# Sparse attention in ten units in place of fourteen: joined local branches, one compressed unit for all heads, values by blocks

## The chip, the cores and the metric

The kernel runs on one core of a Trainium2 chip. The metric is the device time of one execution in microseconds (us). Three runs of the kernel before gave 896.19 to 897.03, median 896.92.

## The reference

Two transformer layers run one after the other on 256 tokens with 1,024 features, in float32. The first (stick-breaking attention, gated linear attention, a feed-forward part) is not touched. In the second the mixing has three branches: sparse attention, a convolution of 31 taps over 512 channels, and attention over 256 memory tokens. Their outputs are gated and added, and a feed-forward part follows. The sparse attention has 8 query heads of 64 features in two groups that share keys and values, and three branches of its own:

```python
s_c = einsum(qq, kc); p_c = masked_softmax(s_c, cmp_end <= t)      # 15 compressed blocks
o_c = einsum(p_c, vc)
...
s_s = einsum(qq, k_g); p_s = masked_softmax(s_s, tok <= t)         # selected blocks
...
s_w = einsum(qq, kwb); p_w = masked_softmax(s_w, m_w)              # window of 512
return gg[..., 0:1] * o_c + gg[..., 1:2] * o_s + gg[..., 2:3] * o_w
```

With 256 tokens there are four blocks to select from and up to 16 may be selected, and the window of 512 covers all that is past. So the selected and the window branch each are causal attention over all tokens, with keys and values of their own; these two are the local branches. The compressed keys and values come from a two-layer network over blocks of 32 tokens.

## The kernel before

All weights pass through a ring of three chunks of 128x2048 elements. SP loads a chunk, ScalarE (ACT) casts it to its high part (`split_hi`, L1383), VectorE (DVE) subtracts to get the low part (`split_lo`, L1984), and TensorE (PE) multiplies high and low parts (three products for each tile; L648 to L650). The second layer's mixing is a loop over steps, one for each chunk, written out for each engine: step s handles chunk number s from `kcvc` on (0 kcvc, 1 ca0, 2 cg0, 3 kk, 4 wk0, 5 q0, 6 wk1, 7 q1, 8 wv0, 9 vv, 10 wv1, 11 ca1, 12 cg1, 13 qm0, 14 qm1, 15 to 24 halves of the gates, 25 to 28 output projections). The chunks `wk` and `wv` (L1109) belong to the compressing network and their products are short; those of the others take about three times as long. In step s an engine first does what the chunk needs and then, in fixed places, pieces of attention and of other small work. Every engine works its queue strictly in that order.

Attention is cut into units, listed in `ATT`; unit i begins in step `ATT_AT + i`, with `ATT_AT` 8. A unit is one branch of one group of four heads for one tile of 128 query tokens (s selected, w window, c compressed), or the memory attention of one tile (m): s, s, w, w, c, c for tile 0, the same for tile 1, then two m, 14 in all. Its pieces are:

- step of the unit: PE's scores (`att_scores`, L1175, m L1167; the mask is added by a product with the identity, L1182); VectorE's maximum over the keys (`att_max_`, L2437, and a small instruction L2438); ScalarE's exponentials with their sums (`att_exp`, L1787, one for each head);
- one step later: reciprocal, gate and scaling of the weights (`att_scale`; VectorE L2445 to L2460, or ScalarE L1796 for the units in `SCALED_BY_ACT`);
- two steps later: PE turns the weights, one block of 128x128 at a time (`att_turn`, L1197); ScalarE copies them out (`att_evac`, L1804);
- three steps later: PE multiplies with the values (`att_values`, L1233, for c L1228, for m L1216), for two units at a time; after the last branch of a tile ScalarE and VectorE write high and low parts of the output (`att_out`, L1815 and L2473).

Scores of all units use the same two PSUM banks, so scores i wait until the exponentials of unit i-1 are done; turns use two other banks and wait for the copy before. VectorE puts the convolution's 124 taps (`conv_taps`, L2494, one 128x256 instruction each) at the end of each step; `TAPS_AT` says how many in which step. On VectorE the order in a step is: scaling of unit i-1, maximum of unit i (in the first two steps of attention these two stand the other way round), normalizations, `split_lo` of the chunk three steps ahead, output, taps. In step 8, 12 it also finishes the hidden product of the compressing network (L2551 to L2553); step 13 on PE projects the compressed values (L1303), and ScalarE copies them out (L1891). In step 15 ScalarE loads another table of functions (L1365).

```python
ATT = [(k, a, g) for a in range(TT) for k in "swc" for g in range(2)] + [("m", a, 0) for a in range(TT)]
SCALED_BY_ACT = (6, 7, 8, 9, 12, 13)
ATT_AT = 8
TAPS_AT = [0, 0, 0, 0, 2, 2, 2, 0, 0, 0, 6, 5, 8, 6, 7, 8, 8, 9, 9, 14, 8, 9, 8, 13]
```

Of the kernel before, what the change touches and what calls it, by code (L numbers as in the profile page):

```python
# [7 lines left out]
F32 = mybir.dt.float32  # L8
# [23 lines left out]
def two_block_kernel(  # L32
# [98 lines left out]
    ATT = [(k, a, g) for a in range(TT) for k in "swc" for g in range(2)] + [("m", a, 0) for a in range(TT)]  # L131
    SCALED_BY_ACT = (6, 7, 8, 9, 12, 13)
    ATT_AT = 8

    with ExitStack() as ctx:
# [136 lines left out]
        vc = AR[0:15, 8854:8982].rearrange("p (g n) -> p g n", g=2)  # L272
# [19 lines left out]
        amax = TMP[:, 4382:4438].rearrange("p (u h) -> p u h", h=4)  # L292
        aden = TMP[:, 4438:4494].rearrange("p (u h) -> p u h", h=4)
        acoef = TMP[:, 4494:4550].rearrange("p (u h) -> p u h", h=4)
# [124 lines left out]
        def key_tiles(i):  # L419
            kind, a, g = ATT[i]  # L420
            return 2 if kind == "m" else 1 if kind == "c" else a + 1

        def group_of(i):

            kind, a, g = ATT[i]
            return 4 + a if kind == "m" else 2 * a + g

        def att_out_bank(i):
            kind, a, g = ATT[i]
            return PS[:, 6 + a, :] if kind == "m" else PS[64 * g:64 * g + 64, 6, :]  # L430
# [82 lines left out]
        def _(pool):  # L513
# [119 lines left out]
            for i in range(2):  # L633
# [8 lines left out]
                               pattern=[[P, TT], [-16, 15]], channel_multiplier=1).then_inc(mask2_made, 1)  # L642

        @block.tensor
        def _(pe):
# [502 lines left out]
            def att_scores(i):  # L1148
                kind, a, g = ATT[i]
                if i >= 1:  # L1150
                    pe.wait_ge(att_e, 4 * i)
# [6 lines left out]
                if i == 4:  # L1158
                    pe.wait_ge(fn_made, 4)
                if i == 12:  # L1160
# [4 lines left out]
                for h in range(4):  # L1165
                    if kind == "m":
                        mm = pe.matmul(PS[:, h // 2, (h % 2) * T:(h % 2) * T + T], qm[:, h, tok], kmT[:, h, :],  # L1167
                                       start=True, stop=True)
                        continue
                    r = slice(64 * (h % 2), 64 * (h % 2) + 64)  # L1170
                    q = qn[r, 2 * g + h // 2, tok]

                    L = 15 if kind == "c" else P * (a + 1)
                    k = kcT[r, 15 * g:15 * g + 15] if kind == "c" else kdup[kind][r, g, 0:L]
                    pe.matmul(PS[:, h % 2, h // 2 * L:(h // 2 + 1) * L], q, k, start=h < 2, stop=False, skip_group_check=True)  # L1175
                if kind != "m":
                    m = mask_r[:, P + 30 * a:P + 30 * a + 30] if kind == "c" else mask_r[:, 0:P].unsqueeze(1).to_broadcast([P, 2, P])
                    for e in range(2):
                        z = PS[:, e, 0:2 * L]
                        if kind != "c":  # L1180
                            z = z.rearrange("p (h n) -> p h n", h=2)[:, :, P * a:P * a + P]
                        mm = pe.matmul(z, ident_r[:, :], m, start=False, stop=True, skip_group_check=True)  # L1182
                mm.then_inc(att_s, 1)

            def att_turn(i):
# [8 lines left out]
                L = 15 if kind == "c" else P  # L1194
                for s in range(key_tiles(i)):
                    for h in range(4):
                        mm = pe.transpose(PS[0:L, 2 + s, h * P:(h + 1) * P],  # L1197
                                          pbuf[:, i % 2, (h * key_tiles(i) + s) * L:(h * key_tiles(i) + s + 1) * L],
                                          ident[:, :])
                mm.then_inc(att_t, 1)  # L1200

            def att_values(i):
# [3 lines left out]
                if kind == "m":  # L1206
                    if a == 0:
                        pe.wait_ge(att_lo, 4)
                    else:
                        pe.wait_ge(vc_made, 1)  # L1210
# [12 lines left out]
                if kind == "s" and a == 1:  # L1223
                    pe.wait_ge(att_lo, 2)
                if kind == "c":
                    pe.wait_ge(vc_made, 1)
                    for w in range(2):
                        pe.matmul(att_out_bank(i - 1 + w), vc[:, w, :], pT[0:15, w, 0:512], start=False, stop=True,  # L1228
                                  skip_group_check=True).then_inc(att_o, 1)
                    return  # L1230
                for s in range(key_tiles(i)):
                    for w in range(2):
                        mm = pe.matmul(att_out_bank(i - 1 + w), vn[kind][:, s, 64 * w:64 * w + 64],  # L1233
                                       pT[:, w, s * 512:(s + 1) * 512], start=kind == "s" and s == 0, stop=False,
                                       skip_group_check=True)
                        if s == key_tiles(i) - 1:
# [15 lines left out]
            for s in range(FFN2 - B2 - 4):  # L1252
# [5 lines left out]
                elif name.startswith("o"):  # L1258
                    br = "mcn".index(name[2])
                    if name[3] == "0":  # L1260
                        if br == 0:
                            pe.wait_ge(att_lo, 6)
                        elif br == 1:
                            pe.wait_ge(cv_lo, 1)
                        else:
                            pe.wait_ge(att_lo, 4)
# [32 lines left out]
                if s == 13:  # L1299
                    pe.wait_ge(h_made, 2)  # L1300
                    for g in range(2):
                        for f in range(2):
                            mm = pe.matmul(PS[0:15, 3, 64 * g:64 * g + 64],  # L1303
                                           hid[1][:, 30 * f + 15 * g:30 * f + 15 * g + 15],
                                           w2v[:, f, :], start=f == 0, stop=f == 1)
# [4 lines left out]
                if 0 <= i < len(ATT) and (ATT[i][0] == "m" or i % 2 == 1):  # L1310
# [3 lines left out]
                if s == 25:  # L1314
                    pe.wait_ge(att_lo, 6)
# [45 lines left out]
        def _(act):  # L1361
# [410 lines left out]
            def att_src(i, h):  # L1772
                kind, a, g = ATT[i]
                L = {"m": T, "c": 15}.get(kind, P * (a + 1))
                if kind == "m":
                    return PS[:, h // 2, (h % 2) * T:(h % 2) * T + T], mpos[:, a, h:h + 1]
                return PS[:, h % 2, h // 2 * L:(h // 2 + 1) * L], qpos[:, a, 4 * g + h:4 * g + h + 1]

            def att_exp(i):
                kind, a, g = ATT[i]  # L1780
# [3 lines left out]
                L = {"m": T, "c": 15}.get(kind, P * (a + 1))  # L1784
                for h in range(4):
                    src, scale = att_src(i, h)
                    act.activation(pbuf[:, i % 2, h * L:(h + 1) * L], src, ACT.Exp, bias=amax[:, i, h:h + 1],  # L1787
                                   scale=scale, accum_out=aden[:, i, h:h + 1]).then_inc(att_e, 1)
# [9 lines left out]
            def att_evac(i):  # L1798
# [4 lines left out]
                L, n = 15 if kind == "c" else P, 512 * key_tiles(i)  # L1803
                act.copy(pT[0:L, i % 2, 0:n], PS[0:L, 2:4, :].rearrange("p b n -> p (b n)")[:, 0:n]).then_inc(att_pt, 1)  # L1804

            def att_out(i):
# [6 lines left out]
                src = att_out_bank(i).rearrange("p (h e t) -> p e h t", h=2, e=2)  # L1813
                for e in range(2):
                    ins = act.copy(oT_hi[64 * e:64 * e + 64, 2 * g:2 * g + 2, tok], src[:, e])  # L1815
# [9 lines left out]
            for n in range(V1, FFN2 - 4):  # L1825
# [63 lines left out]
                if s == 13:  # L1889
                    act.wait_ge(kc_sum, 2)  # L1890
                    act.copy(vc.rearrange("p g n -> p (g n)"), PS[0:15, 3, 0:P]).then_inc(vc_made, 1)  # L1891
# [3 lines left out]
                if 0 <= i < len(ATT) and ATT[i][0] == "m":  # L1895
                    att_out(i)
                if 0 <= i < len(ATT) and ATT[i][0] == "c" and i % 2 == 1:
                    att_out(i - 1)
# [74 lines left out]
        def _(dve):  # L1973
# [451 lines left out]
            def att_max_(i):  # L2425
                kind, a, g = ATT[i]
                dve.wait_ge(fn_made, 7 if kind == "m" else 3 if g else 2)
                dve.wait_ge(att_s, i + 1)
                L = {"m": T, "c": 15}.get(kind, P * (a + 1))
                if kind == "m":  # L2430
                    src, dst = PS[:, 0:2, :].rearrange("p b (h n) -> p (b h) n", n=T), amax[:, i, :]
                    neg = mneg[:, a, :]
                else:
                    src = PS[:, 0:2, 0:2 * L].rearrange("p e (h n) -> p e h n", h=2)
                    dst = amax[:, i, :].rearrange("p (h e) -> p e h", e=2)
                    neg = qneg[:, a, 4 * g:4 * g + 4]
                link(dve.tensor_reduce(dst, src, AX, ALU.max))  # L2437
                dve.scalar_tensor_tensor(amax[:, i, :], amax[:, i, :], -1e29, neg, ALU.max, ALU.mult).then_inc(att_max, 1)  # L2438

            def att_scale(i):  # L2440
                kind, a, g = ATT[i]
                L = {"m": T, "c": 15}.get(kind, P * (a + 1))
                dve.wait_ge(att_e, 4 * i + 4)
                if kind == "c":
                    link(dve.tensor_scalar(aden[:, i, :], aden[:, i, :], 1e-30, None, ALU.max))  # L2445
                if kind == "m":
                    dve.reciprocal(acoef[:, i, :], aden[:, i, :]).then_inc(att_c, 1)
                else:
                    link(dve.reciprocal(aden[:, i, :], aden[:, i, :]))
                    br = "csw".index(kind)  # L2450
                    gate = gn24[:, 24 * a + 12 * g + br:24 * a + 12 * g + br + 10:3]
                    ins = dve.tensor_tensor(acoef[:, i, :], aden[:, i, :], gate, ALU.mult)
# [6 lines left out]
                p = pbuf[:, i % 2, 0:4 * L].rearrange("p (h n) -> p h n", h=4)  # L2459
# [251 lines left out]
```

## Time and profile before

| | us |
|---|---|
| median of three runs | 896.92 |
| profiled execution | 896.35 |
| its span, first to last instruction | 894.6 |
| PE busy | 888.3 (99%) |
| VectorE busy | 624.6 (70%) |
| ScalarE busy | 505.6 (57%) |
| GpSimd (POOL) busy | 84.0 (9%) |

The profiled execution took 1.75 us more than its span, which runs from the first to the last instruction. Attention lies between 507 and 637 us of the span. In the timeline a row is a start, a duration, the engine, the line and the tiles; consecutive alike instructions are merged (xN), and a fp32 product shows as two pieces. Matmuls are pipelined, so the duration of a row on PE reaches a little into the next one, and the difference of two starts is what a group costs.

### The profile page before, as it was taken

To read this page: it belongs to the slowest core of one execution; us is meant where nothing else is said; L and a number is where in the kernel's file an instruction comes from. 1 tells how busy PE (TensorE), PEld (TensorE's weight loads), DVE (VectorE), ACT (ScalarE), POOL (GpSimd) and SP (SyncE) were. 2 spreads that over 40 slices of the span, in tenths; PEclk is the share of its full clock that TensorE was granted. 3 is DMA by queue.
4 is the path that set the end of the run, shared out by engine and by line. 5 is a ranking of instruction groups with operands and counts; after the bars stand their busy time and mean duration, and the time that the engine had idled before them with its cause. 6 is when DMAs were issued, how large, how long until landed. Compare 5 with 4: busy or idle time off the path is not lost.

```text
span 894.6 us, 12610 instructions
## 1 busy us (share of the span) xinstructions
PE 888.3 (99%) x4946; PEld 759.5 (85%) x4946; DVE 624.6 (70%) x795; ACT 505.6 (57%) x703; POOL 84.0 (9%) x154
## 2 busy tenths in 40 slices
PE   9999999999999999999999999999999999999998
PEld 7888888888898888888889988777888888888887
DVE  5656666757776666666686889998886686666664
ACT  6646655545565444444476887987474664444441
POOL 8803332030010000000000000000000000000000
PEclk9999999999999999999999999999999999999999
DMA  8754333486555555555545863443346376556541
GB/s 279 225 188 161 119 125 110 142 274 200 174 152 181 189 191 189 191 191 201 194 147 162 258 194 106 141 142 122 123 172 196 100 234 198 186 194 200 182 163 48
DMA packets 103411, 155.30 MB, mean 174 GB/s; under 512 B 2665, under 2 KB 70353, under 8 KB 103362
## 3 DMA queue, kind: packets, MB, share of 16 engines
q1 hardware_dynamic: 102482, 151.64, 52.0%
q0 software_dynamic: 864, 2.98, 1.0%
q8 instruction: 34, 0.56, 0.3%
q14 instruction: 15, 0.12, 0.0%
q10 hardware_dynamic: 16, 0.00, 0.0%
HBM read 153.57 MB, written 1.05 MB: 173 GB/s over the span
## 4 chain that ended last, share of the span: by engine, by line
PE 94%; ACT 4%; DVE 1%; issue 1%; POOL 0%; ACTq 0%; POOLq 0%
PE PS L648 18%; PE PS L650 18%; PE PS L649 18%; PE PS L1061 15%; PE PS L1066 8%; PE PS L711 3%; PE PS L717 1%; PE PS L946 1%; ACT whi L1383 1%; PE PS L1175 1%; PE PS L1197 1%; PE PS L1233 1%; PE PS L794 1%; ACT TMP L1787 1%; PE PS L1109 1%
## 5 line engine op out<-in xcount | busy, mean ns | idle before, releaser
L1984 DVE TENSOR_TENSOR wlo<-raw,whi 128x2048 fp32r<-128x2048 f32 x141 | 323.2, 2293 | 123.9 <-ACT whi L1383 122.4
L1383 ACT CAST whi<-raw 128x2048 fp32r<-128x2048 f32 x141 | 269.2, 1909 | 110.2 <-PE PS L650 106.9
L1061 PE MATMUL PS<-hT,whi 128*128 128x512 f32 x608 | 144.7, 390 | 0.0
L1061 PEld LDWEIGHTS PS<-hT,whi 128*128 128x128 f32 x608 | 113.1, 188 | 23.2 <-issue 0.2
L648 PE MATMUL PS<-whi,hT 128*128 128x512 f32 (+1 forms) x320 | 126.5, 395 | 0.0
L650 PE MATMUL PS<-whi,hT 128*128 128x512 f32 (+1 forms) x320 | 123.2, 385 | 0.0
L649 PE MATMUL PS<-wlo,hT 128*128 128x512 f32 (+1 forms) x320 | 122.9, 384 | 0.0
L648 PE MATMUL PS<-whi,aT_hi 128*128 128x512 f32 x216 | 84.3, 391 | 0.0
L649 PE MATMUL PS<-wlo,aT_hi 128*128 128x512 f32 x216 | 84.3, 390 | 0.0
L650 PE MATMUL PS<-whi,aT_lo 128*128 128x512 f32 x216 | 84.0, 389 | 0.0
L1066 PEld LDWEIGHTS PS<-hT,wlo 128*128 128x128 f32 x608 | 78.0, 191 | 3.0
L1066 PE MATMUL PS<-hT,wlo 128*128 128x256 f32 x608 | 78.9, 283 | 0.0
L650 PEld LDWEIGHTS PS<-whi,hT 128*128 128x128 f32 x320 | 60.1, 188 | 12.3
L648 PEld LDWEIGHTS PS<-whi,hT 128*128 128x128 f32 x320 | 60.2, 188 | 11.9 <-issue 0.8
L649 PEld LDWEIGHTS PS<-wlo,hT 128*128 128x128 f32 x320 | 60.3, 188 | 11.1
L648 PE MATMUL PS<-hT,whi 128*128 128x256 f32 x176 | 50.8, 289 | 0.0
L649 PE MATMUL PS<-hT,whi 128*128 128x256 f32 x176 | 49.8, 283 | 0.0
L650 PE MATMUL PS<-hT,wlo 128*128 128x256 f32 x176 | 49.8, 283 | 0.0
L2494 DVE SCALAR_TENSOR_TENSOR AR<-AR,cw 128x256 f32<-128x256 f32 x120 | 48.8, 477 | 0.1
L650 PEld LDWEIGHTS PS<-whi,aT_lo 128*128 128x128 f32 x216 | 40.6, 188 | 8.6
L648 PEld LDWEIGHTS PS<-whi,aT_hi 128*128 128x128 f32 x216 | 40.7, 188 | 7.8
L649 PEld LDWEIGHTS PS<-wlo,aT_hi 128*128 128x128 f32 x216 | 40.6, 188 | 7.5
(398 smaller groups left out, 1310.0 us busy)
## 6 DMA issues: line engine op xcount, KB each, us to landing
raw<-in_w_in_dram SPq DMA_DIRECT2D x47, 1024.0 KB, 5.1
raw<-in_w_ff_dram SPq DMA_DIRECT2D x32, 1024.0 KB, 5.5
raw<-in_w_gate_dram SPq DMA_DIRECT2D x11, 1024.0 KB, 5.2
raw<-in_w_up_dram SPq DMA_DIRECT2D x11, 1024.0 KB, 5.2
raw<-in_w_down_dram SPq DMA_DIRECT2D x11, 1024.0 KB, 5.0
raw<-in_w_out_dram SPq DMA_DIRECT2D x8, 1024.0 KB, 4.9
raw<-in_w_proj_gla_dram SPq DMA_DIRECT2D x4, 1024.0 KB, 6.1
raw<-in_w_mem_kv_dram SPq DMA_DIRECT2D x4, 1024.0 KB, 5.1
```

Source lines behind the costliest of these rows:

```text
L648: pe.matmul(dst, a_hi, b_hi, start=start, stop=False, skip_group_check=True)
L649: pe.matmul(dst, a_hi, b_lo, start=False, stop=False, skip_group_check=True)
L650: return pe.matmul(dst, a_lo, b_hi, start=False, stop=stop, skip_group_check=True)
L711: pe.matmul(PS[:, b + c, :], w_hi[:, k, c * P:(c + 1) * P], hT[:, k, :, :].rearrange("p w t -> p (w t)"), start=k == 0, stop=False, skip_g ...
L717: mm = pe.matmul(PS[:, b + c, 0:T], w_lo[:, k, c * P:(c + 1) * P], hT_hi[:, k, :], start=False, stop=k == KT - 1, skip_group_check=True)
L794: pe.matmul(PS[:, bank, 0:P], ident[:, :], ident[:, :], start=True, stop=True)
L946: mm = pe.matmul(o, QK[:, l, :], q, start=True, stop=True)
L1061: pe.matmul(PS[:, bank + c, :], w_hi[:, k, c * P:(c + 1) * P], hT[:, k, :, :].rearrange("p w t -> p (w t)"), start=k == 0, stop=False, ski ...
L1066: mm = pe.matmul(PS[:, bank + c, 0:T], w_lo[:, k, c * P:(c + 1) * P], hT_hi[:, k, :], start=False, stop=k == KT - 1, skip_group_check=True)
L1383: act.copy(whi[:, n % RING, :], raw[:, n % RING, :]).then_inc(hi_made, 1)
L1984: dve.tensor_tensor(wlo[:, n % RING, :], raw[:, n % RING, :], whi[:, n % RING, :].bitcast(F32), ALU.subtract).then_inc(lo_made, 1)
L2494: ins = dve.scalar_tensor_tensor(cacc[:, f, :], src, cw[:, f, k:k + 1], cacc[:, f, :], ALU.mult, ALU.add)
```

## The change

- For tile 0 the selected and the window branch of a group become one unit (kind b): the scores of a head are one product with both branches' 128 keys each, eight rows of weights per unit. Two units in place of four.
- For both tiles the compressed branch of all eight heads becomes one unit: the scores stay separate products of 15 columns, but the weights stand in one 128x128 block, 15 columns for each head with a place of their own, so that a single turn does for all heads.
- The compressed values are written eight times, once for each place, with zeros elsewhere: four products (one for each block of 32 rows, over all 30 columns of both groups) in place of two, and VectorE multiplies the result with a mask of ones and zeros (`own_block`) in place of ScalarE's copy. The values of unit c are then four products of 128 columns with full rows.
- 10 units in place of 14, starting at step 10 in place of 8. `TAPS_AT` is laid out anew. The sum of taps stays 124.
- POOL makes `own_block` with three more instructions at the end of its constants; maxima, sums and coefficients have moved in memory.

```diff
-    ATT = [(k, a, g) for a in range(TT) for k in "swc" for g in range(2)] + [("m", a, 0) for a in range(TT)]
-    SCALED_BY_ACT = (6, 7, 8, 9, 12, 13)
-    ATT_AT = 8
+    ATT = [("b", 0, 0), ("b", 0, 1), ("c", 0, 0)] + [(k, 1, g) for k in "sw" for g in range(2)] + [("c", 1, 0)] + \
+          [("m", a, 0) for a in range(TT)]
+    SCALED_BY_ACT = (3, 4, 5, 6, 8, 9)
+    ATT_AT = 10
...
+        def heads(i):
+            return 8 if ATT[i][0] in "bc" else 4
...
             def att_scores(i):
                 if i >= 1:
-                    pe.wait_ge(att_e, 4 * i)
+                    pe.wait_ge(att_e, exps_before(i))
...
+                elif kind == "c":
+                    for x in range(4):
+                        for e in range(2):
+                            r = slice(64 * e, 64 * e + 64)
+                            d, z = x // 2, x % 2
+                            pe.matmul(PS[:, e, 15 * x:15 * x + 15], qn[r, 2 * z + d, tok], kcT[r, 15 * z:15 * z + 15], ...)
...
+                else:
+                    for h in range(4):
+                        r = slice(64 * (h % 2), 64 * (h % 2) + 64)
+                        k = kboth[r, :, g, 0:P] if kind == "b" else kdup[kind][r, g, :]
+                        pe.matmul(PS[:, h % 2, h // 2 * T:(h // 2 + 1) * T], qn[r, 2 * g + h // 2, tok], k, ...)
...
             def att_turn(i):
+                else:
+                    pe.wait_ge(h_raw, 2)
+                if kind == "c":
+                    mm = pe.transpose(PS[:, 2, 0:P], pbuf[:, i % 2, 0:P], ident[:, :])
...
             def att_values(i):
                 if i == 1:
+                    pe.wait_ge(vc_made, 1)
...
                 if kind == "c":
+                    for h in range(4):
+                        mm = pe.matmul(PS[:, 6, h * P:(h + 1) * P], vcb[:, 2 * h:2 * h + 2, :].rearrange("p g n -> p (g n)"),
+                                       pT[:, i % 2, 0:P], start=False, stop=True, skip_group_check=True)
...
                 if s == 13:
                     pe.wait_ge(h_made, 2)
-                    for g in range(2):
+                    for b in range(4):
                         for f in range(2):
+                            mm = pe.matmul(PS[32 * b:32 * b + 30, 6, 0:64], hid[1][:, 30 * f:30 * f + 30], w2v[:, f, :], ...)
...
-            TAPS_AT = [0, 0, 0, 0, 2, 2, 2, 0, 0, 0, 6, 5, 8, 6, 7, 8, 8, 9, 9, 14, 8, 9, 8, 13]
+            TAPS_AT = [0, 0, 0, 0, 2, 2, 2, 2, 5, 5, 5, 4, 4, 4, 6, 7, 7, 8, 8, 14, 9, 10, 10, 10]
...
+                if s == 13:
+                    dve.wait_ge(kc_sum, 2)
+                    dve.wait_ge(mask2_made, 6)
+                    dve.tensor_tensor(vcb, PS[:, 6, 0:64].unsqueeze(1).to_broadcast([P, 8, 64]),
+                                      own_block.unsqueeze(2).to_broadcast([P, 8, 64]), ALU.mult).then_inc(vc_made, 1)
```

In the new list, values are multiplied for units 0 and 1 together in step 14 (after `vcb` is there), for unit 2 (c) in step 15, for units 3 and 4 in step 17, 5 and 6 in step 19, 7 (c) in step 20, and the two m in steps 21 and 22. The maximum of kinds b and c needs two small instructions behind the reduction in place of one. Units 3 to 6 and the m units are scaled by ScalarE, as their likes were before.

## Rows read from the trace of the kernel before

**Rows 1.** The page: PE's busy time, share, instructions; clock granted in 40 slices (tenths).

```profile
PE 888.3 (99%) x4946; PEld 759.5 (85%) x4946; DVE 624.6 (70%) x795; ACT 505.6 (57%) x703; POOL 84.0 (9%) x154
...
PEclk9999999999999999999999999999999999999999
```

**Rows 2.** Timeline of PE, step 10 (start, duration, line, tiles; idle before and releaser).

```profile
517.34 0.28 PE L1109 MATMUL PS<-wlo,aT_lo 128*66 128x256 f32 x1
517.81 0.65 PE L1197 MATMUL PS<-ident,TMP 128*128 128x128 f32 x4 [0.19 <-DVE TMP L2460]
518.75 0.71 PE L1175 MATMUL PS<-AR 64*128 64x128 f32 x8 [0.28 <-ACT TMP L1787]
```

**Rows 3.** Timeline of PE, end of step 12.

```profile
534.00 0.60 PE L1197 MATMUL PS<-ident,TMP 128*128 128x128 f32 x4
534.53 1.08 PE L1233 MATMUL PS<-TMP,AR 128*64 128x512 f32 x4
535.54 0.62 PE L1175 MATMUL PS<-AR 64*128 64x15 f32 x8
```

**Rows 4.** Timeline of PE, end of step 8 to the end of step 11.

```profile
507.63 0.71 PE L1175 MATMUL PS<-AR 64*128 64x128 f32 x8
...
508.42 0.36 PE L648 MATMUL PS<-whi,hT 128*128 128x256 f32 x1
...
525.95 0.64 PE L1197 MATMUL PS<-ident,TMP 128*128 128x128 f32 x4
```

**Rows 5.** Timeline of PE, steps 13, 15 and 17 to 18.

```profile
542.08 0.62 PE L1303 MATMUL PS<-w2v,AR 128*15 128x64 f32 x8
...
560.54 0.60 PE L1197 MATMUL PS<-ident,TMP 128*15 128x128 f32 x4
...
577.75 1.13 PE L1175 MATMUL PS<-AR 64*128 64x256 f32 x8
...
578.96 0.48 PE L648 MATMUL PS<-whi,hT 128*128 128x512 f32 x1
...
584.52 1.04 PE L1197 MATMUL PS<-ident,TMP 128*128 128x128 f32 x8
585.49 1.94 PE L1233 MATMUL PS<-TMP,AR 128*64 128x512 f32 x8
```

**Rows 6.** Timeline of VectorE, steps 8 to 19.

```profile
510.89 0.68 DVE L2437 TENSOR_REDUCE TMP<-PS 128x4 f32<-128x512 f32 x1
...
513.48 2.29 DVE L1984 TENSOR_TENSOR wlo<-raw,whi 128x2048 fp32r<-128x2048 f32 x1
...
523.89 2.46 DVE L2494 SCALAR_TENSOR_TENSOR AR<-AR,cw 128x256 f32<-128x256 f32 x6
...
541.45 0.22 DVE L2553 TENSOR_TENSOR AR<-AR 128x60 f32<-128x60 f32 x1
...
556.31 1.22 DVE L2437 TENSOR_REDUCE TMP<-PS 128x4 f32<-128x1024 f32 x1
...
597.93 5.63 DVE L2494 SCALAR_TENSOR_TENSOR AR<-AR,cw 128x256 f32<-128x256 f32 x14
```

**Rows 7.** Timeline of ScalarE, steps 8 to 16.

```profile
511.81 0.46 ACT L1787 ACTIVATE TMP<-PS,TMP 128x128 f32<-128x128 f32 x1 [0.95 <-DVE TMP L2438]
...
513.48 0.21 ACT L1787 ACTIVATION_READ_ACCUMULATOR TMP<-PS,TMP 128x1 f32 x1
...
561.24 1.28 ACT L1365 ACT_TABLE_LOAD   x1
...
564.35 1.70 ACT L1796 ACTIVATE TMP<-TMP 128x256 f32<-128x256 f32 x4
...
572.96 1.50 ACT L1815 CAST oT_hi<-PS 64x256 fp32r<-64x256 f32 x4
574.48 1.02 ACT L1804 COPY TMP<-PS 128x1024 f32<-128x1024 f32 x1
...
577.48 0.21 ACT L1787 ACTIVATION_READ_ACCUMULATOR TMP<-PS,TMP 128x1 f32 x1
```

More of the change, by code:

```diff
@@ L1164, in att_scores @@
                 tok = slice(a * P, (a + 1) * P)
-                for h in range(4):
-                    if kind == "m":
+                if kind == "m":
+                    for h in range(4):
                         mm = pe.matmul(PS[:, h // 2, (h % 2) * T:(h % 2) * T + T], qm[:, h, tok], kmT[:, h, :],
                                        start=True, stop=True)
[L1169 to L1175, printed above, removed]
@@ L1222, in att_values @@
                     pe.wait_ge(drained[unit_of["vv"] % 2], unit_of["vv"] // 2 + 1)
-                if kind == "s" and a == 1:
-                    pe.wait_ge(att_lo, 2)
+                    pe.wait_ge(vc_made, 1)
+                if kind == "s":
+                    pe.wait_ge(att_lo, 1)
                 if kind == "c":
-                    pe.wait_ge(vc_made, 1)
-                    for w in range(2):
[L1228 to L1236, printed above, removed]
+                    for h in range(4):
+                        mm = pe.matmul(PS[:, 6, h * P:(h + 1) * P], vcb[:, 2 * h:2 * h + 2, :].rearrange("p g n -> p (g n)"),
+                                       pT[:, i % 2, 0:P], start=False, stop=True, skip_group_check=True)
+                    mm.then_inc(att_o, 1)
+                    return
+                for s in range(2):
+                    for w in range(2):
+                        v = vn["sw"[s]][:, 0, 64 * w:64 * w + 64] if kind == "b" else vn[kind][:, s, 64 * w:64 * w + 64]
+                        mm = pe.matmul(att_out_bank(i - 1 + w), v, pT[:, (i - 1 + w) % 2, s * 512:(s + 1) * 512],
+                                       start=kind in "bs" and s == 0, stop=False, skip_group_check=True)
+                        if s == 1:
                             mm.then_inc(att_o, 1)
@@ L1783, in att_exp @@
                     act.wait_ge(att_t, i - 1)
[L1784 to L1788, printed above, removed]
+                for x in range(heads(i)):
+                    src, scale, to = att_src(i, x)
+                    act.activation(pbuf[:, i % 2, to], src, ACT.Exp, bias=amax[:, i, x:x + 1],
+                                   scale=scale, accum_out=aden[:, i, x:x + 1]).then_inc(att_e, 1)
             def att_scale(i):
@@ L1812, in att_out @@
                     return
-                src = att_out_bank(i).rearrange("p (h e t) -> p e h t", h=2, e=2)
-                for e in range(2):
-                    ins = act.copy(oT_hi[64 * e:64 * e + 64, 2 * g:2 * g + 2, tok], src[:, e])
+                for g in range(2):
+                    src = PS[64 * g:64 * g + 64, 6, :].rearrange("p (h e t) -> p e h t", h=2, e=2)
+                    for e in range(2):
+                        ins = act.copy(oT_hi[64 * e:64 * e + 64, 2 * g:2 * g + 2, tok], src[:, e])
                 ins.then_inc(att_hi, 1)
```

179 lines of the change are left out of this document (108 added, 71 removed).

## The prediction, made before the changed kernel was built or run

> **What bounds the kernel now.** I read the page's busy shares first, then TensorE's timeline from 505 to 650 us, where the attention units lie, then VectorE's and ScalarE's of the same stretch. PE is busy 99% of the span at an unbroken granted clock [rows 1], so what counts is PE's own work and its waits, and I cost PE by start-to-start times (a merged row's duration has a tail of some 0.07 us). In the attention stretch PE waits mainly in one place, step 10: the products of chunk wv1 issue their last piece at 517.34, due to be followed 0.12 later, but the first turn starts at 517.81 (0.35 lost, VectorE's scaling of unit 0 was late); that turn is followed by scores 0.94 later in place of 0.53 (0.4 lost, the exponentials of unit 1 were late) [rows 2, 3]. A further 0.2 lies before the scores of unit 9. So 0.95 us is all that better timing could give; the rest must come from fewer PE instructions.
>
> **PE work removed and added.** First tile, local branches: four units of scores at 0.79 (507.63 to 508.42) [rows 4] become two whose matmuls have the second tile's 256 columns, 1.21 (577.75 to 578.96) [rows 5], and a mask of 512 columns where that one has 256, some 0.2 more (two instructions; 128 more columns cost the scores' eight pieces 1.06 - 0.64, 0.05 each): 2 x 1.42 for 4 x 0.79, -0.3. Four turns of four blocks at 0.53 become two of eight at 0.97 [rows 3, 5]: -0.2. Two values groups of 1.01 become one of 1.87 (1.94 less the tail): -0.15 [rows 3, 5]. Compressed branch, both tiles: four units of scores at 0.62 become two with twice the matmuls, -0.05 at a row's price per matmul (0.62 less the tail for four; the small mask adds little) [rows 3]. Four turns at 0.53 become two of one block; four blocks cost 0.53 and eight 0.97, so one is 0.2: -1.7. It lies between 0.11 (the slope) and 0.53 (no saving); I take 0.2. Values: two groups of 1.0 (two matmuls of 512 columns, as in the 1.01) become two of four matmuls in eight pieces of 128 columns, priced like the turn's eight blocks, 0.95: -0.1 [rows 3, 5]. The compressed values' projection grows from four small matmuls to eight, +0.55 (the 0.62 at 542.08 less the tail) [rows 5]. Sum: **-2.0 us** of PE work (-1.4 if the short turns save only half, -2.3 at the slope).
>
> **What costs nothing.** ScalarE's exponentials stay 56 in number; it loses some turn copies and the copy of the compressed values. That copy becomes a VectorE product of 128x512 (0.7 like the reduction of that size [rows 6]); PE needs it one step later, after a step of products (5.56, 578.96 to 584.52 [rows 5]), and without that cover it would cost its 0.7. POOL's three new instructions stand at the end of its queue, behind nothing that waits, long before their reader. No DMA moves; SP's loads follow VectorE's splits as before.
>
> **The new wait.** Unit 0's scores move from step 8 to the end of step 10, behind the short chunk wv1, and unit 1's to the end of step 11. Scores 1 may start only when all eight exponentials of unit 0 are done, since they use the same banks. When does PE want it? In the trace it goes from 508.42 to 525.95 for the products of steps 9, 10 and 11 with their small extras [rows 4], 17.53, which holds two groups of scores (1.58), one turn (0.55) and 0.75 of waits: 14.65 net. Now it starts at 507.63 (no scores in step 8) and adds the new scores 0 (1.42): PE is ready for scores 1 at 523.7.
>
> VectorE is later. Its queue has unit 0's maximum behind step 9's split and taps, and the taps of steps 7 to 10 rise from 0, 0, 0, 6 to 2, 5, 5, 5. In the trace the split of step 8 starts at 513.48, after unit 0's reduction and what follows it [rows 6]; in the new order two taps (0.4 each, from six in 2.46) take the place of the reduction and its follower (0.8), so it still starts at 513.48. Then: split 2.2 to 515.7, five taps 2.0 to 517.7, split of step 9 to 519.9, five taps to 521.9; only now the maximum: reduction of 1,024 elements 1.2, and two small instructions (0.2 each, like 541.45's, partly overlapped): 523.4 [rows 6]. The exponentials: four take 1.88 from the first start to the last accumulator's end (511.81 to 513.69), eight 3.65 [rows 7]: done at 527.05. PE waits 527.05 - 523.7 = **+3.4 us**. Nothing behind it on PE can pass: step 12's products are queued after it, so the whole kernel moves. The scores themselves are there at 517.5, so the ten taps of steps 8 and 9 (4.0) are what makes it late.
>
> **Smaller waits.** (a) Step 13's projection of the compressed values needs VectorE's hidden product of step 12. In the trace that product is done 0.4 before PE reads it (541.68 and 542.08) [rows 5, 6]; in the same queue unit 1's scaling and unit 2's maximum now take some 0.85 more: +0.5 (0 to 0.9). (b) Step 15 on ScalarE: table load at 561.24, scaling at 564.35 to 566.0, then now output copies, a turn copy of 1,024 and four exponentials, which in the trace follow each other in the next step and take 4.7 (572.96 to 577.69): 570.7 in the trace's time. PE is through with step 15's products and sums at 560.54 and then needs turn 0.97, values 0.95, scores 1.21, step 16's products 5.56 and a turn 0.97 until it wants the next scores at 570.2: +0.5 (0 to 1) [rows 5, 7]. (c) Step 19's 14 taps (5.6) hold back unit 9's coefficients: counted from scores 9, maximum and wait 1.8, split 2.2, taps 5.6, coefficients 0.2, ScalarE's scaling 1.6, output copies 1.5, turn copy 0.9 make 13.8 against PE's 5.56 + 0.97 + 0.95 + 5.56 = 13.05: +0.7 (0 to 1) [rows 5 to 7].
>
> **Sum.** -2.0 - 0.95 + 3.4 + 0.5 + 0.5 + 0.7 = **+2.15 us**. The profiled execution took 896.35 (span 894.6), which makes 898.5; the median of the runs shown is 896.92, 0.57 above it, so I forecast 899.0 (899.07). Behind step 27 both kernels have the same work and PE the same order, so nothing is given back there. Some 0.2% (1.8 us) is what a measurement of this kernel can tell from no change: the forecast lies just beyond it.
>
> **Rivals.** *VectorE is not late at step 10* (not slower). If the ten taps do not stand between PE's scores 0 and its scores 1, because VectorE catches up somewhere in steps 7 to 9, then the maximum starts at 517.5, exponentials end by 522.7, and PE finds them ready; (a) falls with it. The point is 518.5: a maximum that starts by then costs nothing. The sum is -2.95 + 0.5 + 0.7 = -1.75: 895.2. For it: in the trace it reached this maximum 2.5 us after the scores' end (508.42 and 510.89) [rows 4, 6], and step 9's products are long enough to let it catch up in part. Against: splits and taps run strictly in order, each as long as its row, and the short step 10 gives no time back. Chance 0.1.
>
> *Only the large wait, the small ones vanish* (no measurable change). (a) to (c) each rest on a difference of under 1 us between sums of ten terms. Without them +0.45: 897.4. With one of them, +0.95 to 1.15. Chance 0.27.
>
> *The wait also slows the clock* (slower still). In this stage no row shows PE idle for longer than 0.3 us at a time, and the granted clock never falls [rows 1, 2]; a wait of 3.4 us is new. If the granted clock fell to its 1.2 GHz level for part of the next step, products of 5.56 would take up to twice as long: between 0 and 5.6, middle 2.8, so 901.8. The page "TensorE: Matmul & The Clock Gate" of the Trainium skill (section "The HAM clock gate") has it that an idle TensorE is put to half rate and is given full rate only after it has been busy again; no row here can show it. Chance 0.07, since VectorE and ScalarE, which gain from a slow PE, would meanwhile catch up and remove waits (b) and (c).
>
> **How the numbers follow.** Forecast 0.56; rivals 0.1, 0.27, 0.07. The likeliest case by itself spans 898.0 to 900.2 from the bounds of the turns and of (a) to (c). The range takes in the second rival and part of the others: 896.5 to 901.2. Faster by over 0.2%: some half of the first rival and a little, 0.07. Within: the second rival, the rest of the first and the low end of the forecast, 0.35. Slower: the rest of the forecast and the third rival, 0.58.
>
> **What would show it.** In the changed profile: scores of unit 1 with some 3.4 us of PE idle before them, released by ScalarE's exponentials, and those released by VectorE's maximum, which stands right behind five taps; the granted clock unbroken; short gaps before the values' projection, before scores 6 and before turn 9; the attention groups of PE some 2 us shorter in sum. The prediction is wrong if the maximum of unit 0 starts before 518.5, if the one-block turns cost as much as four, or if a wait stands elsewhere, at the blocked values above all.

## The result and the profile after

The changed kernel took 899.54 us (median of seven runs, 898.03 to 901.49), the kernel before 896.44 (seven runs, 896.18 to 897.03): 1.0036 times as long, interval 1.0027 to 1.0045, so 3.1 us slower. The profiled execution took 899.75, its span is 898.0. In the code of the changed kernel the scores of kinds b, s and w are L1200, those of c L1190, turns L1228 (c L1223), values L1263 (c L1256, m L1244), the projection of the compressed values L1332, the exponentials L1820, the turn copies L1837, the maximum L2472 with its small instructions at L2474 and L2476, the taps L2549, the splits L2012.

The page first: busy times and the clock, as in [rows 1].

```profile
PE 886.3 (99%) x4924; PEld 759.2 (85%) x4924; DVE 624.2 (70%) x778; ACT 504.0 (56%) x698; POOL 84.0 (9%) x157
...
PEclk9999999999999999999999999999999999999999
```

PE is busy 2.0 us less, with 22 instructions fewer, and yet the span is 3.4 longer: the time went into waits. The clock row looks unbroken, but one of its 40 slices is 22 us long. Second, the waits of PE (line that waited, releaser; us in total, times, longest); the kernel before had none above 0.3 us in this stage. A wait of 1.9 us behind POOL at the start of the kernel is in both. The one of L834 lies some 8 us into the kernel, far ahead of the attention, and no other trace of this case has it.

```profile
PE PS L1200 <- ACT TMP L1820: 4.1, 3, 3.1
...
PE PS L1228 <- ACT TMP L1837: 1.0, 1, 1.0
PE PS L834 <- DVE AR L2230: 0.5, 1, 0.5
PE PS L1332 <- DVE AR L2608: 0.4, 1, 0.4
```

In the attention, scores wait for exponentials three times, a turn for a turn copy, the projection for the hidden product. PE's timeline shows where. The rows answer to [rows 2, 3, 5].

```profile
516.19 1.13 PE L1200 MATMUL PS<-AR 64*128 64x256 f32 x8
517.26 0.61 PE L1207 MATMUL PS<-mask_r,ident_r 128*128 128x512 bf16 x2
517.51 0.47 PE L664 MATMUL PS<-hT,whi 128*128 128x256 f32 x1
...
523.80 0.39 PE L1148 MATMUL PS<-TMP,negtri 128*128 128x30 f32 x2
527.28 1.63 PE L1200 MATMUL PS<-AR 64*128 64x256 f32 x8 [3.09 <-ACT TMP L1820]
528.85 1.04 PE L1207 MATMUL PS<-mask_r,ident_r 128*128 128x512 bf16 x2
529.32 0.78 PE L664 MATMUL PS<-hT,whi 128*128 128x256 f32 x1
...
536.10 1.02 PE L1148 MATMUL PS<-xn,negone 128*128 128x512 f32 x2
...
537.92 1.07 PE L1190 MATMUL PS<-AR 64*128 64x15 f32 x16
...
545.39 0.45 PE L1332 MATMUL PS<-w2v,AR 128*30 128x64 f32 x16 [0.41 <-DVE AR L2608]
545.78 1.09 PE L1228 MATMUL PS<-ident,TMP 128*128 128x128 f32 x8
547.38 1.13 PE L1200 MATMUL PS<-AR 64*128 64x256 f32 x8 [0.51 <-ACT TMP L1820]
...
555.29 0.27 PE L1223 MATMUL PS<-ident,TMP 128*128 128x128 f32 x1
555.49 1.94 PE L1263 MATMUL PS<-TMP,AR 128*64 128x512 f32 x8
...
576.03 1.13 PE L1200 MATMUL PS<-AR 64*128 64x256 f32 x8 [0.48 <-ACT TMP L1820]
...
618.10 1.06 PE L1228 MATMUL PS<-ident,TMP 128*128 128x128 f32 x8 [0.99 <-ACT TMP L1837]
```

Where nothing waits, scores 1 start 0.31 behind the sums that stand here at 523.80 (experiment 2 below); here they start 3.48 behind them, a wait of 3.17. Four small waits follow: before the projection (0.69 from the start ahead of it), before scores 3 (1.60), before scores 6 (1.52) and before turn 9 (1.38). The same distances in experiment 8, where none of them waits, are 0.21, 1.03, 0.97 and 0.23, so the waits are 0.48, 0.57, 0.55 and 1.15.

Behind the main wait something else is odd: the scores of unit 1 take 1.57 (527.28 to 528.85), those of unit 0 1.07; the products of step 12 take 6.78 (529.32 to 536.10), those of step 11 5.93 (517.51 to 523.44). The busy time by stretches says why (us, then busy time of PE, PEld, DVE, ACT, POOL with instructions, then the granted clock, DMA share, GB/s).

```profile
523.80:527.28 3.48, 0.39 (x4) 0.28 (x3) 3.48 (x6) 3.48 (x17) 0.00 (x0) 1.00 0.41 111
527.28:529.32 2.04, 2.04 (x10) 1.04 (x11) 0.78 (x4) 1.98 (x6) 0.00 (x0) 0.62 0.91 327
529.32:531.31 1.99, 1.99 (x11) 1.90 (x9) 1.60 (x4) 1.51 (x2) 0.00 (x0) 0.53 0.42 161
531.31:536.10 4.79, 4.79 (x43) 4.79 (x41) 4.62 (x11) 3.63 (x16) 0.00 (x0) 1.00 0.00 0
```

PE had nothing to do for 3 us, and then, with work again, it was granted 0.62 and 0.53 of full speed for 4 us: its 1.2 GHz level for most of that. At half speed the pieces of step 12 take 0.21 in place of 0.12. Read from starts, the fall cost 0.50 in the scores, 0.21 in the mask and 0.85 in the products: 1.56 us.

What made scores 1 late is in VectorE's timeline of steps 8 to 11, which answers to [rows 6]:

```profile
513.70 2.29 DVE L2012 TENSOR_TENSOR wlo<-raw,whi 128x2048 fp32r<-128x2048 f32 x1
515.91 2.06 DVE L2549 SCALAR_TENSOR_TENSOR AR<-AR,cw 128x256 f32<-128x256 f32 x5
517.89 2.29 DVE L2012 TENSOR_TENSOR wlo<-raw,whi 128x2048 fp32r<-128x2048 f32 x1
520.09 2.06 DVE L2549 SCALAR_TENSOR_TENSOR AR<-AR,cw 128x256 f32<-128x256 f32 x5
522.07 1.22 DVE L2472 TENSOR_REDUCE TMP<-PS 128x8 f32<-128x1024 f32 x1
...
523.40 0.16 DVE L2476 SCALAR_TENSOR_TENSOR TMP<-TMP 128x4 f32<-128x4 f32 x1
```

and in ScalarE's, which answers to [rows 7], the first and the last of the eight exponentials of unit 0 (each is an ACTIVATE and an accumulator read):

```profile
523.60 0.46 ACT L1820 ACTIVATE TMP<-PS,TMP 128x128 f32<-128x128 f32 x1 [4.96 <-DVE TMP L2476]
...
527.00 0.23 ACT L1820 ACTIVATION_READ_ACCUMULATOR TMP<-PS,TMP 128x1 f32 x1
```

The scores of unit 0 were complete at 517.9; VectorE reached them at 522.07, behind two groups of five taps. ScalarE had idled 4.96 us for them, ended the exponentials at 527.23, and PE went on at 527.28.

So the books of the profiled execution close: touched PE groups -3.26 (below), old waits gone -0.95, five new waits +5.92, slow clock +1.56: +3.3, where the two profiled executions differ by 899.75 - 896.35 = 3.4.

### The profile page after: what moved, and what is told of

Same layout as the page of the kernel before. It is cut to its first block, busy times and chain, and to the rows that moved or that the text cites. A ratio compares the mean times of both kernels' runs of the same rounds, so it can differ in the third digit from the quotient of the medians.

```text
span 898.0 us, 12531 instructions
## 1 busy us (share of the span) xinstructions
PE 886.3 (99%) x4924; PEld 759.2 (85%) x4924; DVE 624.2 (70%) x778; ACT 504.0 (56%) x698; POOL 84.0 (9%) x157
## 3 DMA queue, kind: packets, MB, share of 16 engines
HBM read 153.57 MB, written 1.05 MB: 172 GB/s over the span
## 4 chain that ended last, share of the span: by engine, by line
PE 89%; ACT 5%; DVE 4%; issue 1%; DMA 0%; ACTq 0%; DVEq 0%
PE PS L664 17%; PE PS L666 17%; PE PS L665 17%; PE PS L1077 15%; PE PS L1082 8%; PE PS L727 3%; PE PS L733 1%; DVE wlo L2012 1%; PE PS L962 1%; DVE AR L2549 1%; ACT whi L1411 1%; ACT TMP L1820 1%; PE PS L1263 1%; PE PS L904 1%; PE PS L1200 1%
## 5 line engine op out<-in xcount | busy, mean ns | idle before, releaser
L2012 DVE TENSOR_TENSOR wlo<-raw,whi 128x2048 fp32r<-128x2048 f32 x141 | 324.6, 2304 | 122.2 <-ACT whi L1411 120.7
L2549 DVE SCALAR_TENSOR_TENSOR AR<-AR,cw 128x256 f32<-128x256 f32 x120 | 49.1, 478 | 0.1
```

Source lines behind the costliest of these rows:

```text
L2012: dve.tensor_tensor(wlo[:, n % RING, :], raw[:, n % RING, :], whi[:, n % RING, :].bitcast(F32), ALU.subtract).then_inc(lo_made, 1)
L2549: ins = dve.scalar_tensor_tensor(cacc[:, f, :], src, cw[:, f, k:k + 1], cacc[:, f, :], ALU.mult, ALU.add)
```

## The experiments

Ten kernels. The kernel before took 896.52 (27 runs) beside the first four, 896.43 (18 runs) beside the next four and 896.43 (7 runs) beside the last two.

**1. Keep PE busy in the wait.** Twelve transposes without a reader, into a free bank, fill most of the wait before scores 1.

```diff
             def att_scores(i):
                 kind, a, g = ATT[i]
+                if i == 1:
+                    keep_warm(2, 12)
                 if i >= 1:
                     pe.wait_ge(att_e, exps_before(i))
```

> The changed kernel, with 12 products of 128x128 into an unused bank put on PE just ahead of the wait before scores 1 (2.7 us of the 3.3 us wait). Theory (the wait lets the granted clock fall to 1.2 GHz behind it, which costs some 1.6 us): scores 1 start at the same 527.3, the granted clock stays at 1.00 from 527 to 531, time 897.9 to 898.1, and the runs lie closer together than the changed kernel's 898.0 to 901.5. Rival (the slow products behind the wait come from something else that begins there, such as the chunk load that moves 327 GB/s in that stretch): the products stay at 0.21 us a piece, time 899.5 as before.

Measured: 898.18 (11 runs, 897.87 to 898.71), ratio to the kernel before 1.002, interval 1.0011 to 1.0029. The timeline and the clock by stretches of this kernel (its line numbers are 2 higher):

```profile
524.54 2.92 PE L810 MATMUL PS<-ident 128*128 128x128 f32 x24
527.77 1.13 PE L1202 MATMUL PS<-AR 64*128 64x256 f32 x8 [0.31 <-ACT TMP L1822]
528.84 0.60 PE L1209 MATMUL PS<-mask_r,ident_r 128*128 128x512 bf16 x2
```

```profile
527.77:529.10 1.33, 1.33 (x11) 0.83 (x11) 0.47 (x2) 1.30 (x4) 0.00 (x0) 1.00 0.90 296
529.10:531.31 2.21, 2.21 (x19) 2.18 (x18) 1.77 (x4) 2.18 (x4) 0.00 (x0) 1.00 0.68 262
```

From the sums to scores 1 it takes as long as before (524.31 to 527.77, 3.46); PE only does idle work meanwhile. Yet scores 1 take 1.07 again and the clock stays at 1.00. The DMA is as busy as in the changed kernel (0.90 of the engines against 0.91), so it isn't traffic that slowed the scores. Between the medians the slow clock costs 899.54 - 898.18 = 1.36 us. It also makes most of the spread of the changed kernel: of its seven runs the one with a mean granted clock of 1.000 took 898.03, the four at 0.997 to 0.998 took 899.32 to 899.75, the two at 0.996 took 900.92 and 901.49. The page "TensorE: Matmul & The Clock Gate" of the Trainium skill (section "HAM oscillation — how this bites in real kernels") describes the same for a loop that waits for its loads: the wait itself is paid, and then half rate on the work behind it. The rows here agree, for one single wait (a granted clock of 0.62 and 0.53 behind it).

**2. No taps in steps 8 and 9.** The ten taps go to later steps.

```diff
-            TAPS_AT = [0, 0, 0, 0, 2, 2, 2, 2, 5, 5, 5, 4, 4, 4, 6, 7, 7, 8, 8, 14, 9, 10, 10, 10]
+            TAPS_AT = [0, 0, 0, 0, 2, 2, 2, 2, 0, 0, 5, 4, 4, 6, 8, 9, 9, 10, 8, 14, 9, 10, 10, 10]
```

> The changed kernel with the ten taps of steps 8 and 9 moved to steps 13 to 17. Theory (the taps alone make unit 0's maximum late): the wait of 3.3 us before scores 1 is gone, the clock does not fall; the waits of steps 13, 16 and 21 stay (0.6 + 0.6 + 0.55 + 1.1); 899.5 - 3.3 - 1.5 = 894.7, faster than the kernel before by 1.7. Rival (eight exponentials in a row and the joined maximum are too long for step 11 whatever the taps): a wait of 2 us or more stays before scores 1, time 897.5 or above.

Measured: 895.13 (11 runs, 894.68 to 895.56), ratio 0.9985 (0.9976 to 0.9994). PE's timeline, then VectorE's maximum of unit 0:

```profile
524.36 0.39 PE L1148 MATMUL PS<-TMP,negtri 128*128 128x30 f32 x2
524.67 1.13 PE L1200 MATMUL PS<-AR 64*128 64x256 f32 x8
```

```profile
519.00 1.22 DVE L2472 TENSOR_REDUCE TMP<-PS 128x8 f32<-128x1024 f32 x1
```

The maximum comes 3.07 earlier than in the changed kernel, and scores 1 find everything done. The median falls by 4.4 against the changed kernel: the wait of 3.17 and the slow clock behind it (1.36 by experiment 1) make 4.5. The other four waits are still there.

**3. No taps in step 9 alone.**

```diff
-            TAPS_AT = [0, 0, 0, 0, 2, 2, 2, 2, 5, 5, 5, 4, 4, 4, 6, 7, 7, 8, 8, 14, 9, 10, 10, 10]
+            TAPS_AT = [0, 0, 0, 0, 2, 2, 2, 2, 5, 0, 5, 4, 4, 4, 7, 8, 8, 9, 9, 14, 9, 10, 10, 10]
```

> The changed kernel with only the five taps of step 9 moved to steps 14 to 18. Theory: the wait before scores 1 shrinks by the taps' 2.0 us to 1.3, and a wait of that length leaves the clock at 1.00: 899.5 - 2.0 - 1.5 = 896.0. Rival (any new wait lowers the clock, or the wait is not the taps'): 897.5 (clock low at 1.3 us of wait) or 899.5.

Measured: 896.32 (11 runs, 895.77 to 896.70), ratio 0.9999 (0.9990 to 1.0008).

```profile
524.87 1.13 PE L1200 MATMUL PS<-AR 64*128 64x256 f32 x8 [1.11 <-ACT TMP L1820]
```

Five taps, 2 us of VectorE, shorten PE's wait by 2 us (1.18 by starts in place of 3.17). The mean granted clock was 0.999 to 1.000 in all eleven runs, as in the kernel before: this wait costs itself and no more.

**4. The old units with the new taps.** The kernel before, with the `TAPS_AT` of the change and nothing else.

```diff
-            TAPS_AT = [0, 0, 0, 0, 2, 2, 2, 0, 0, 0, 6, 5, 8, 6, 7, 8, 8, 9, 9, 14, 8, 9, 8, 13]
+            TAPS_AT = [0, 0, 0, 0, 2, 2, 2, 2, 5, 5, 5, 4, 4, 4, 6, 7, 7, 8, 8, 14, 9, 10, 10, 10]
```

> The kernel before, 14 units from step 8, with the tap layout of the changed kernel and nothing else. Theory (the layout by itself makes VectorE late in steps 8 to 10, whatever the units): a wait of some 3 us before the first turn in step 10, time 896.4 + 2.6 = 899.0, and 1 to 2 us more where the clock falls. Rival (the layout costs only with joined units): 896.4 to 896.9.

Measured: 900.15 (5 runs, 899.40 to 900.75), ratio 1.0043 (1.0029 to 1.0057). The profiled execution, PE's timeline and the clock by stretches:

```profile
517.97 0.28 PE L1109 MATMUL PS<-wlo,aT_lo 128*66 128x256 f32 x1
520.89 0.66 PE L1197 MATMUL PS<-ident,TMP 128*128 128x128 f32 x4 [2.64 <-DVE TMP L2460]
```

```profile
518.25:520.89 2.64, 0.00 (x0) 0.00 (x1) 2.54 (x8) 1.03 (x5) 0.00 (x0) 1.00 0.96 312
520.89:523.00 2.11, 1.88 (x17) 1.50 (x18) 2.11 (x2) 2.11 (x6) 0.00 (x0) 1.00 0.30 97
```

The same taps make the old kernel slower too, by 3.6: here the first turn waits, for VectorE's scaling of unit 0. In the profiled execution (899.40) and one more (899.46) the clock stayed whole; in the other three its mean was 0.998 and they took 900.15 to 900.75. So this layout of the taps makes VectorE late by itself; it needs no joined units for that. Only the execution of 899.40 has a trace, so how long PE waited in the other four isn't shown.

**5. The new units with the old taps.** The other half of the change alone.

```diff
-            TAPS_AT = [0, 0, 0, 0, 2, 2, 2, 2, 5, 5, 5, 4, 4, 4, 6, 7, 7, 8, 8, 14, 9, 10, 10, 10]
+            TAPS_AT = [0, 0, 0, 0, 2, 2, 2, 0, 0, 0, 6, 5, 8, 6, 7, 8, 8, 9, 9, 14, 8, 9, 8, 13]
```

> The changed kernel with the tap layout of the kernel before (none in steps 7 to 9, eight in step 12) and nothing else. Theory: no wait before scores 1, since VectorE is free in steps 8 and 9, but 8 and 6 taps in steps 12 and 13 make VectorE's blocked values late, so a new wait of some 1.2 us comes before the first values (unit 1, step 14); the other small waits stay: 895.1 + 1.1 = 896.2. Rival (the new layout was needed nowhere): no wait at the values, 895.1.

Measured: 896.17 (11 runs, 895.46 to 896.51), ratio 0.9995 (0.9986 to 1.0004). No wait before scores 1, but a new one in step 14. PE, then VectorE:

```profile
550.04 0.27 PE L1223 MATMUL PS<-ident,TMP 128*128 128x128 f32 x1
551.30 1.51 PE L1263 MATMUL PS<-TMP,AR 128*64 128x512 f32 x6 [1.00 <-DVE AR L2648]
```

```profile
542.93 3.25 DVE L2549 SCALAR_TENSOR_TENSOR AR<-AR,cw 128x256 f32<-128x256 f32 x8
...
550.47 0.69 DVE L2648 TENSOR_TENSOR AR<-PS,TMP 128x512 f32<-128x512 f32 x1
```

With eight taps in step 12 the product with `own_block` (L2648) ends at 551.16 and the values of unit 1 start 1.06 late. With that wait and the small ones the joined units gain nothing that can be told: about 3.8 us of waits eat their 4.3. So neither tap layout fits the new units: the old one is late for the values, the new one for scores 1.

**6. Also take away the waits of step 13.** The taps of experiment 2; and in step 12 VectorE's normalization of the keys goes behind the scaling and the maximum in place of ahead of them.

```diff
-                if s in FN_AT:
+                if s in FN_AT and s != 12:
                     e = FN_AT.index(s)
                     (key_norm if e in KEYS else query_norm)(e)
...
                 if 1 < s - ATT_AT < len(ATT):
                     att_max_(s - ATT_AT)
+                if s == 12:
+                    key_norm(FN_AT.index(s))
```

> The kernel with the ten taps moved to steps 13 to 17, and in step 12 VectorE scales unit 1 and takes unit 2's maximum ahead of the key normalization in place of behind it. Theory (the waits before the values' projection and before scores 3 are one chain, VectorE's order in step 12): both go, but for some 0.2; 895.1 - 1.0 = 894.1. Rival (ScalarE's eight exponentials of unit 2 set them): 894.9 to 895.1.

Measured: 893.98 (8 runs, 893.38 to 894.55), ratio 0.9973 (0.9962 to 0.9983). The waits before the projection and before scores 3 are gone. Against experiment 2 the median falls by 1.15; the two waits were 0.48 + 0.57 = 1.05. One change of order removes both because VectorE stood idle ahead of that normalization, with unit 1's scaling and unit 2's maximum queued behind it (the changed kernel):

```profile
540.17 0.69 DVE L2426 SCALAR_TENSOR_TENSOR xn<-PS,xn 128x512 f32<-128x512 f32 x1 [1.21 <-ACT xn L1791]
```

There the maximum of unit 2 started at 543.87, though its scores were complete at 539.15. In this experiment it starts at 535.70, ahead of the normalization at 536.16, and VectorE no longer idles there.

**7. Also spread the 14 taps of step 19.**

```diff
-            TAPS_AT = [0, 0, 0, 0, 2, 2, 2, 2, 0, 0, 5, 4, 4, 6, 8, 9, 9, 10, 8, 14, 9, 10, 10, 10]
+            TAPS_AT = [0, 0, 0, 0, 2, 2, 2, 2, 0, 0, 5, 4, 4, 6, 8, 9, 9, 11, 11, 10, 9, 10, 10, 10]
```

> The kernel with the ten taps moved and the new order in step 12, and step 19's 14 taps cut to 10 (the others in steps 17 and 18). Theory (the taps of step 19 hold back unit 9's coefficients, ScalarE's scaling of it holds back the copy that turn 9 waits for): the wait of 1.1 us before turn 9 goes, 894.1 - 1.0 = 893.1. Rival (ScalarE's own queue in step 20 is the limit): the wait stays at 0.5 or more, 893.6 to 894.1.

Measured: 892.72 (5 runs, 892.52 to 893.26), ratio 0.9958 (0.9944 to 0.9972). Turn 9 no longer waits: 1.26 less than experiment 6, for a wait of 1.15.

**8. Also free the scores of step 16.** In step 15 ScalarE copies the output after the exponentials, and VectorE does its taps ahead of the output's low part.

```diff
-                if 0 <= i < len(ATT) and ATT[i][0] in "mc":
+                if 0 <= i < len(ATT) and ATT[i][0] in "mc" and s != 15:
                     att_out(i)
...
                 if 0 <= s - ATT_AT < len(ATT):
                     att_exp(s - ATT_AT)
+                if s == 15:
+                    att_out(i)
```

> As the one with 10 taps in step 19, and in step 15 ScalarE writes unit 2's output behind unit 5's exponentials in place of ahead of them (VectorE takes its taps of that step ahead of its part of the output). Theory (ScalarE's queue of step 15 is what scores 6 wait for): that wait of 0.55 us goes, 893.1 - 0.5 = 892.6, no new wait. Rival (VectorE's later output delays what follows it): 893.1 or more, with a wait before turn 5 or the values of unit 4.

Measured: 892.13 (5 runs, 891.90 to 892.82), ratio 0.9953 (0.9939 to 0.9966). This one beats both kernels: 4.3 us below the kernel before, 7.4 below the changed one. Its waits of PE, the whole list:

```profile
PE PS L810 <- POOL eps L541: 1.9, 1, 1.9
PE PS L1148 <- ACT xn L1768: 0.3, 1, 0.3
```

Both were there before the change. With no wait left in the stage, the change is worth 4.3 us: 0.95 of old waits, and the rest, 3.35, PE's work (3.26 by starts in the traces, below). Whether the old kernel could be rid of its 0.95 by better timing alone was not tried.

**9 and 10. The price of the projection.** It costs 0.39 (545.39 to 545.78) for 16 pieces where 8 cost 0.55 before [rows 5]. Two copies of experiment 8 have sixteen more pieces ahead of it, whose results nobody reads; in one all write to the same 30 rows, in the other they go round the four blocks of 32 rows.

```diff
+                    for b in range(4):
+                        for f in range(2):
+                            pe.matmul(PS[0:30, 6, 64 + 64 * (b % 3):128 + 64 * (b % 3)], hid[1][:, 30 * f:30 * f + 30], w2v[:, f, :],
+                                      start=f == 0, stop=f == 1)
```

> The version with all waits removed, plus eight more projection matmuls (16 pieces) ahead of the eight of step 13; all of the added ones write to the same 30 rows of PSUM, in unused columns that nobody reads. It prices a piece that writes to one row block. Theory: the projection costs 0.39 in place of the forecast 1.1 because its pieces go to four different blocks of 32 rows, and such pieces overlap; then the 16 added ones, all in one block, cost what the 8 of the kernel before did, 0.069 each, 1.1 in all, and the group with the old ones 1.4 to 1.5. Rival: these pieces are just cheap with 30 columns of weights (0.024 each), wherever they write: then 0.4 more, the group 0.75 to 0.8.

```diff
-                            pe.matmul(PS[0:30, 6, 64 + 64 * (b % 3):128 + 64 * (b % 3)], hid[1][:, 30 * f:30 * f + 30], w2v[:, f, :],
+                            pe.matmul(PS[32 * b:32 * b + 30, 6, 64 + 64 * (b % 3):128 + 64 * (b % 3)], hid[1][:, 30 * f:30 * f + 30], w2v[:, f, :],
```

> The same sixteen added pieces, but spread over the four blocks of 32 rows, two matmuls in a row each, as the projection itself does it. Both theories expect 0.4 more than without them, the group 0.75 to 0.8; if it is 1.4 or more, neither holds, and the low price of the projection belongs to its place (its pieces would then overlap with the group behind it).

PE's timeline in the two kernels (L1332 the added pieces, L1336 the projection), one block first:

```profile
540.01 1.08 PE L1332 MATMUL PS<-w2v,AR 128*30 128x64 f32 x16
540.93 0.44 PE L1336 MATMUL PS<-w2v,AR 128*30 128x64 f32 x16
541.30 1.09 PE L1228 MATMUL PS<-ident,TMP 128*128 128x128 f32 x8
```

```profile
540.30 0.45 PE L1332 MATMUL PS<-w2v,AR 128*30 128x64 f32 x16
540.54 0.44 PE L1336 MATMUL PS<-w2v,AR 128*30 128x64 f32 x16
540.92 1.09 PE L1228 MATMUL PS<-ident,TMP 128*128 128x128 f32 x8
```

The same sixteen pieces cost 0.92 into one block and 0.24 into four, so pieces for different blocks overlap. The sizes were a little off: 0.92 in place of the 1.1, 0.24 in place of 0.4 (the projection alone takes 0.38 there, 0.14 more than the added group; that the group behind it, which writes to all 128 rows, doesn't overlap with it is a guess). The page "TensorEngine Tiling (Array Packing)" of the Trainium skill (section "Key Properties") says that different tiles, the parts into which the array can be cut, work in parallel. These rows agree: 0.92 / 0.24 is a factor of 3.8 for four blocks. The medians, 893.02 and 892.50 (4 runs each; ratios 0.9960, 0.9941 to 0.9980, and 0.9956, 0.9937 to 0.9976), stand in the same order, but their ranges touch.

## Why the prediction was right, and where it was not

The forecast was 899.0; 899.54 was measured, inside the range and on the likeliest side. The mechanism at its centre was right. That the number came so near is in part luck. As a difference, +2.15 was forecast and +3.1 measured; half of that gap is hidden because the kernel before came out at 896.44 in place of the 896.92 that the forecast started from. And the errors in the sum are larger than what they leave: PE's work 1.26 lower, the waits together 0.8 higher, the clock 1.4 higher.

**The main wait** was forecast as 3.4 and measured as 3.17, by the very chain that the prediction walked: maximum at 521.9 forecast, 522.07 measured; its small instructions done at 523.4, and 523.56; exponentials done at 527.05, and 527.23; PE ready at 523.7, and 524.1. Experiments 2 and 3 show that the ten taps make it, each group of five 2 us. Experiment 4 shows that it needs no joined units.

**PE's work: the term that was mis-sized most.** Forecast -2.0. Summed from starts, the touched groups take 14.47 in the kernel before (its first turn, which a wait blurs, taken at 0.53) and 11.21 in experiment 8, where no wait blurs them: -3.26. The step that failed is "the compressed values' projection grows from four small matmuls to eight, +0.55": it shrank by 0.17, since eight matmuls were priced by their number and not by where they write (experiments 9 and 10). That is 0.72 of the 1.26. The c scores brought 0.34 in place of 0.05 (1.07 for eight heads against two times 0.62), the b scores 0.52 in place of 0.3 (1.32 each, not 1.42), the c values 0.22 in place of 0.1. The turns were nearly as forecast: one block costs 0.20 (555.29 to 555.49).

**The small waits.** Forecast (a) 0.5, (b) 0.5, (c) 0.7; measured 0.48, 0.55, 1.15, each at the place named. One was not forecast: 0.57 before scores 3, a wait elsewhere, which the prediction itself had named as a sign of being wrong. It has the same root as (a): VectorE does the scaling of unit 1 and the maximum of unit 2 behind the key normalization of step 12, so the exponentials of unit 2 come late too. The list of VectorE's order in a step that stands ahead of the prediction has this wrong: it puts the normalizations behind the maximum, but in both kernels they stand ahead of the scaling (540.17 and 543.87 above). In the listed order, which is what experiment 6 makes of step 12, the wait is gone. The prediction followed the queue to the hidden product and not on to the exponentials. PE also came 0.72 earlier than forecast, out of a cheap projection; by the sum, the wait of 0.57 would otherwise have been covered. Experiments 6, 7 and 8 take these waits away, and the medians fall by 1.15, 1.26 and 0.59.

**The clock** was to stay unbroken by the prediction's own signs; its fall was a rival with a chance of 0.07, and it came true in six of seven runs. The reason against it, that VectorE and ScalarE would catch up, weighed small waits and not the fall itself. Its price, taken as the middle of 0 to 5.6, was 2.8; the median run paid 1.36, the longest some 3.3 (901.49 against 898.18). Without it the kernel takes 898.0 to 898.2, still slower than before by 1.6 to 1.7: the sum without the clock is -3.26 - 0.95 + 5.92 = +1.7, which agrees, and lies 0.4 below the forecast's +2.15.

**The rivals that fell.** VectorE did not catch up in steps 7 to 9: the maximum started at 522.07, where 518.5 was the point. The small waits did not vanish. The values of the blocked unit, named as the wait that would disprove the forecast, do not wait in the changed kernel (555.49, right behind the turn); they do under the old taps (experiment 5), so that cover is real but thin.

**Open.** Why one run in seven kept its clock stays open: no trace of that run is kept, so its wait isn't shown, and nothing was tried on it.

## What to carry to other kernels

A change that removes work of the bounding engine is worth that work only if the small jobs which other engines put between its steps are laid out anew for the new due times: here 3.3 us less work, with optional work ahead of a due maximum, came out as 3.1 us lost, and as 4.3 gained once five waits were taken out one by one. Follow a late engine's queue to every one of its readers, since one late block makes several waits. And a TensorE wait can cost more than itself, as the one of 3.2 us did here: a few idle products in its place are a cheap way to learn how much of the loss is the clock.

## What the runs showed of the hardware that was not expected

- One wait in the midst of a kernel can lower the granted clock for the work behind it: in the traced run of the changed kernel to 0.62 and then 0.53 of full speed for 4 us, behind 3.1 us of idle time. By the mean clock of each run the fall came in six runs of seven of that kernel, in three of five of the one whose trace has 2.64 us of idle time (the traced run itself kept its clock), and in none of eleven of the one whose trace has 1.11 us. Products without a reader in the wait kept it at 1.00.
- Small products that write to four different blocks of 32 rows overlap: 0.015 us a piece against 0.058 into one block.
- The profile page's clock row, with slices of 22 us, did not show the fall of 4 us; windows of 2 us did.
